# Expert inputs picked by matmuls with a zero-one matrix, in place of indirect gathers and transposes, in a one-core encoder step

## What is computed

```
g_idx = jnp.argmax(g_logits, axis=-1)                       # 1 of 4 groups
top_v, top_i = lax.top_k(e_sel, TOP_K_INNER)                # 2 of its 4 experts
top_w = jax.nn.softmax(top_v, axis=-1) * g_w
combine = jnp.sum(one_hot(e_idx, N_EXPERTS) * top_w[..., None], axis=1)
for e in range(N_EXPERTS):                                  # 16
    h = jax.nn.silu(xt @ w_gate[e]) * (xt @ w_up[e])        # 1024 -> 512
    y = y + combine[:, e:e + 1] * (h @ w_down[e])           # 512 -> 1024
```

## Time and profile before

| | us |
|---|---|
| Median of 3 runs | 639.69 (635.85 to 643.37) |
| The profiled execution, its own time | 645.62 |
| Its span, first to last instruction | 643.8 |
| Busy in the span: PE / PEld / DVE / ACT / POOL | 531.8 / 393.8 / 229.8 / 130.2 / 71.1 |
| Granted TensorE clock, mean of the span | 0.919 |
| Read from HBM in the execution | 146.14 MB |

### The profile page before, as it was taken

How to read it: one execution, slowest core, us unless ns; L and a number is a source line. 1 busy time by engine, 2 the same in 40 slices (tenths; PEclk the granted TensorE clock), 3 DMA queues, 4 the chain that set the end, 5 groups by cost and what they waited for, 6 DMA issues and landing times.

```text
span 643.8 us, 9041 instructions
## 1 busy us (share of the span) xinstructions
PE 531.8 (83%) x3544; PEld 393.8 (61%) x3545; DVE 229.8 (36%) x487; ACT 130.2 (20%) x240; POOL 71.1 (11%) x88
## 2 busy tenths in 40 slices
PE   1299979999999999999992699978987789787740
PEld 1299965987888897968772456544554455444310
DVE  5623985685344222213336111121111111111177
ACT  1424359654423122100020000000000000000010
POOL 4590400000000000010000700010000000000210
PEclk9999998977999999999975599998988999989795
DMA  7696541212135887891066269999999999999632
GB/s 216 193 235 224 150 131 54 84 61 65 34 131 186 312 281 273 285 329 69 33 254 252 80 255 374 389 398 393 390 386 412 409 408 406 409 424 424 236 122 82
DMA packets 55353, 158.53 MB, mean 246 GB/s; under 512 B 3572, under 2 KB 35792, under 8 KB 51216
## 3 DMA queue, kind: packets, MB, share of 16 engines
q1 hardware_dynamic: 46320, 135.11, 55.9%
q0 software_dynamic: 4896, 13.92, 8.0%
q10 hardware_dynamic: 4096, 8.92, 3.8%
HBM read 146.14 MB, written 11.78 MB: 245 GB/s over the span
## 4 chain that ended last, share of the span: by engine, by line
PE 61%; DMA 20%; DVE 7%; issue 4%; ACT 3%; SPq 3%; DVEq 0%; POOL 0%; POOLq 0%; ACTq 0%
PE bank L1015 19%; DMA expert_slots<-in_w_up 10%; PE bank L825 8%; PE bank L976 7%; PE bank L812 6%; PE bank L814 6%; PE bank L813 6%; DMA expert_slots<-in_w_in 5%; PE bank L901 3%; SPq L591 2%; PE bank L1008 2%; DMA z_rows<-work 2%; PE bank L881 1%; DVE work L1384 1%; DMA expert_slots<-expert_rows,slot_i 1%
## 5 line engine op out<-in xcount | busy, mean ns | idle before, releaser
L1015 PE MATMUL bank<-expert_slots,work 128*64 128x256 f32 (+3 forms) x1584 | 191.7, 416 | 26.1 <-DMA expert_slots<-in_w_gate 11.1
L1015 PEld LDWEIGHTS bank<-expert_slots,work 128*64 128x64 f32 (+1 forms) x1584 | 106.7, 139 | 100.0 <-issue 45.8
L812 PE MATMUL bank<-z_high,weights_high 128*128 128x320 f32 (+1 forms) x256 | 81.5, 318 | 0.6 <-DVE weights_low L532 0.6
L813 PE MATMUL bank<-z_low,weights_high 128*128 128x320 f32 (+1 forms) x256 | 79.9, 312 | 0.0
L814 PE MATMUL bank<-z_high,weights_low 128*128 128x320 f32 (+1 forms) x256 | 79.8, 312 | 0.0
L1720 DVE SCALAR_TENSOR_TENSOR work<-work,bank 128x256 f32<-128x256 f32 (+1 forms) x18 | 7.3, 406 | 144.0 <-ACT work L1296 138.1
L532 DVE TENSOR_TENSOR weights_low<-expert_slots,weights_high 128x2048 fp32r<-128x2048 f32 x18 | 41.2, 2287 | 34.0 <-ACT weights_high L527 34.0
L825 PE MATMUL bank<-work,expert_slots 128*128 128x320 f32 x192 | 52.3, 432 | 0.0
L812 PEld LDWEIGHTS bank<-z_high,weights_high 128*128 128x128 f32 x256 | 48.9, 191 | 1.9 <-DVE weights_low L532 1.1
L813 PEld LDWEIGHTS bank<-z_low,weights_high 128*128 128x128 f32 x256 | 48.6, 190 | 0.2
L814 PEld LDWEIGHTS bank<-z_high,weights_low 128*128 128x128 f32 x256 | 48.5, 189 | 0.0
(11 more groups left out here) (249 smaller groups left out, 590.8 us busy)
## 6 DMA issues: line engine op xcount, KB each, us to landing
expert_slots<-in_w_gate SPq DMA_DIRECT2D x16, 2048.0 KB, 25.0
expert_slots<-in_w_up SPq DMA_DIRECT2D x16, 2048.0 KB, 29.6
expert_slots<-in_w_down SPq DMA_DIRECT2D x15, 2048.0 KB, 23.5
expert_slots<-in_w_in SPq DMA_DIRECT2D x19, 1024.0 KB, 5.6
expert_slots<-in_w_branch_rnn SPq DMA_DIRECT2D x4, 1024.0 KB, 7.3
expert_slots<-in_w_out SPq DMA_DIRECT2D x4, 1024.0 KB, 5.7
expert_rows<-work ACTq DMA_DIRECT2D x30, 128.0 KB, 8.2
expert_rows<-work POOLq DMA_DIRECT2D x6, 384.0 KB, 9.3
```

What stands on the lines that cost most here:

```text
L812: nc.tensor.matmul(b[:, 0:NALL - lo], wh[:, k, o], zh[:, k, lo:NALL], start=(k == 0), stop=False)
L813: nc.tensor.matmul(b[:, 0:NALL - lo], wh[:, k, o], zl[k // 4][:, k % 4, lo:NALL], start=False, stop=False)
L1015: mm = nc.tensor.matmul(bank[m * j:m * j + m, cols], lhsT(k), rhs(k, j), start=(k == 0), stop=(k == kk - 1))
```

## The change

- `gather`, `turn` and the copies `columns` for the 16 experts go. TensorE forms an expert's input in `choose`: `rows` (stationary, every eighth column) times a matrix `pick` of tokens x places, zero or one, that VectorE makes (`pick_item`) from the token's rank plus one if it chose the expert (`pick_rank`). The product is already transposed. Only the first 64 places are made always; `choose_rest` makes the other 32 within the branch.
- `columns` copies one bank of 512 columns; `rest_columns` is added in the branch.
- The ranks take three matmuls in place of nine.
- The token index is made later (`overflow_index`), behind expert 0's turn of hidden, since only overflow items still gather.
- On VectorE `columns(0, 0)` stands amid the routing arithmetic; `pick_item(1)` and `(2)` behind the control words; its expert loop is written out; pick i + 3 is made behind `hidden_columns`.
- The multiplication of `rows` by ALPHA moves from Pool, early in the stage, to ACT, behind the last expert's tanh, because `rows` are now read until then. ACT waits for `ctrl_done` in its first step, not for `route_done` ahead of it.

```diff
-            for i in range(NE):
-                if i >= 3:
-                    pool.wait_ge(xt_full, i - 2)
-                gather(i, i % 3)
-                if i == 2:
-                    scale_residual()
...
-            for j in range(3):
-                for i in range(j):
-                    nc.tensor.matmul(b[:, NE * j:NE * j + NE], ones, e_sum[:, i, :], start=(i == 0), stop=False)
-                nc.tensor.matmul(b[:, NE * j:NE * j + NE], before, e_sum[:, j, :], start=(j == 0), stop=True)
-            for i in range(3):
-                mm = nc.tensor.matmul(b[:, NE * 3:NE * 4], ones, e_sum[:, i, :], start=(i == 0), stop=(i == 2))
...
+            nc.tensor.matmul(b[:, 0:NE], before, e_sum[:, 0, :], start=True, stop=True)
+            nc.tensor.matmul(b[:, NE:4 * NE], ones, e_upto.rearrange(flat), start=True, stop=False)
+            nc.tensor.matmul(b[:, NE:3 * NE], before, e_sum[:, 1:3, :].rearrange(flat), start=False, stop=True)\
+                .then_inc(S.f_full("ranks"), 1)
...
+            def picked(bank, s, at, n):
+
+                for k in range(KD):
+                    for j in range(3):
+                        m = OUT_ROWS[j]
+                        z = rows[0:m, j, :].rearrange("t (p k) -> t k p", k=KD)
+                        mm = nc.tensor.matmul(bank[:, n * k:n * k + n], z[:, k, :], pick[s][0:m, j, at:at + n],
+                                              start=(j == 0), stop=(j == 2))
+                return mm
+
+            def choose(i, s):
+
+                pe.wait_ge(pick_made, i + 1)
                 wait_past(pe, xt_made, i)
+                picked(TB[0], s, 0, FIRST).then_inc(xt_full, 1)
+
+            def choose_rest(s, b):
+
+                picked(TB[1], s, FIRST, REST).then_inc(xr_full, 1)
+                pe.wait_ge(xr_made, b + 1)
...
                     hidden(i, s, n, ha_full)
                     if not (first and s == 0):
                         down(i - 1, (s - 1) % 3, n if s else n - 1)
-                    turn(i + 1, (s + 1) % 3, n + (s + 1) // 3)
+                    choose(i + 1, (s + 1) % 3)
+                    if first and s == 0:
+                        pe.wait_ge(ctrl_done, 1)
+                    if first and s == 1:
+                        pe.wait_ge(route_done, 1)
                     maybe_rest(i, s, n)
                     turn_hidden(ha_made, i + 1, hta_full)
-
-            turn(0, 0, 0)
+                    if first and s == 0:
+                        overflow_index()
+
+            choose(0, 0)
...
+            for j in range(3):
+                n = OUT_ROWS[j]
+                nc.scalar.mul(rows[0:n, j, :], rows[0:n, j, :], ALPHA).then_inc(rows_scaled2, 1)
...
+            def pick_item(i):
+
+                slot = cst("iota_cap").unsqueeze(1).to_broadcast([P, 3, CAP])
+                mine = pick_rank[:, :, i].unsqueeze(2).to_broadcast([P, 3, CAP])
+                stt(pick[i % 3], slot, 1.0, mine, ALU.add, ALU.is_equal).then_inc(pick_made, 1)
+
+            def columns(i, s):
+                dve.wait_ge(xt_full, i + 1)
+                V.tensor_copy(xT[s][:, :, 0:FIRST], TB[0][:, :].rearrange("p (k c) -> p k c", c=FIRST)).then_inc(xt_made, 1)
```

More of the change, by code:

```diff
@@ L233, in pe_fills @@
         s += [(kind, j, h) for h in range(2)]
-    s += ["ranks", "index"]
+    s.append("ranks")
     return m, s
@@ L350, in build @@
         ea = Area(work, 3 * D, NWORK)
-        xg = [ea.take(D) for _ in range(3)]
+        pick = [ea.take(3, CAP) for _ in range(3)]
+        xg = ea.take(D)
         xT = [ea.take(KD, CAP) for _ in range(3)]
@@ L384, in build @@
         br = sb("router_bias", [1, 20])
-        rt = Area(work, 3 * D + KD * (NALL + META) + KD * NTOK + 4 * NTOK, NWORK)
+        rt = Area(work, max(ea.at, 3 * D + KD * (NALL + META) + KD * NTOK + 4 * NTOK), NWORK)
         logit = rt.take(3, 20)
-        e_sum = rt.take(3, NE)
+        e_sum, e_upto = rt.take(3, NE), rt.take(3, NE)
         rank_hot = rt.take(2, 3 * CAP)
@@ L393, in build @@
         own = sm.take(2, 3)
+        pick_rank = sm.take(3, NE)
         idle = sm.take(1)
@@ L991, in _ @@
-            pe.wait_ge(selected, 1)
-            b = S.claim(pe, "index")
-            for k in range(2):
-                for j in range(3):
-                    mm = nc.tensor.matmul(b[0:CAP, 0:NITEM], rank_hot[:, k, CAP * j:CAP * j + CAP], item_hot[:, k, NITEM * j:NITEM * j + NITEM],
-                                          start=(k == 0 and j == 0), stop=(k == 1 and j == 2))
-            mm.then_inc(S.f_full("index"), 1)
-            pe.wait_ge(route_done, 1)
-            def turn(i, s, n):
-                pe.wait_ge(xg_in[s], 16 * (n + 1))
-                wait_past(pe, xt_made, i)
-                cols = xg[s][0:CAP, :].rearrange("c (p k) -> c k p", k=KD)
+            flat = "p j e -> p (j e)"
@@ new lines, in _, with overflow_index @@
+            nc.tensor.matmul(b[:, 0:NE], before, e_sum[:, 0, :], start=True, stop=True)
+            nc.tensor.matmul(b[:, NE:4 * NE], ones, e_upto.rearrange(flat), start=True, stop=False)
+            nc.tensor.matmul(b[:, NE:3 * NE], before, e_sum[:, 1:3, :].rearrange(flat), start=False, stop=True)\
+                .then_inc(S.f_full("ranks"), 1)
+            def overflow_index():
+                pe.wait_ge(selected, 1)
+                for k in range(2):
+                    for j in range(3):
+                        mm = nc.tensor.matmul(TB[1][0:CAP, 0:NITEM], rank_hot[:, k, CAP * j:CAP * j + CAP],
+                                              item_hot[:, k, NITEM * j:NITEM * j + NITEM],
+                                              start=(k == 0 and j == 0), stop=(k == 1 and j == 2))
+                mm.then_inc(index_full, 1)
@@ L1336, in round_of @@
                         rows_out(i - 1, (s - 1) % 3, n if s else n - 1, i - 1)
+                    if first and s == 0:
+                        act.wait_ge(ctrl_done, 1)
                     maybe_rest(i)
@@ L1668, in _ @@
             step.settle()
+            columns(0, 0)
             alone(stt(base, ov_end, float(NE - 1), ov, ALU.add, ALU.subtract))
@@ L1783, in _ @@
             with dve.If(has > 0):
+                rest_columns(0, b)
                 rest(b + count)
```

80 lines of the change are left out of this document (45 added, 35 removed).

## The result

The changed kernel takes 869.75 us (861.56 to 870.67, 4 runs) beside 641.53 us (635.85 to 644.36, 4 runs) of the kernel before, measured on the same chip: a ratio of 1.353, 95% interval 1.346 to 1.359. The direction was as predicted, the size was not: 714 us had been forecast, with 738 as the upper end.

What follows compares the result with a forecast made beforehand. TensorE's pace was taken to bound the early expert stage, the weight stream the later. 86.1 + 15.5 - 26.7 - 1.4 = +73.5 us, added to the median 639.7, gave 713.2, plus 1 more: 714, range 668 to 738.

Steps and rivals of the forecast that it cites:

- Price of one choose: TensorE's 48 records forming one expert's input: 7.55 us against 1.07 for the transposes before; 6.9 us for a rest.
- the first of the three prices: In a choose, each record's load of 128 columns was to take 107 to 112 ns, taken from L954.
- rival C: Choose loads pay for reading every eighth word: 224 ns a load, 13.1 us a choose, 812 us in all; chance 0.12.
- The clock: Expert matmuls in each step of the stage were priced at 10.56 us, with a choose of 7.55 at full clock.
- Start of the stage: Ranks to expert 1: choose(0) 10.2 us, 5.3 of it at half clock; expert 1 at 373.9 instead of 375.30, saving 1.4.
- the change of rows: In a choose, switching between 128 and 64 rows adds about 40 ns and leaves the second record's load unhidden: 200, then 160.
- the copy: VectorE's copy behind each choose: one of 512 columns, 0.78 us instead of 1.10.
- the tail behind expert 14: From the end of expert 14's down matmuls to the end of the span: 45 us, as before.
- ScalarE's scaling: Residual scaling moved behind the last tanh, ending at 616.3, costed at nothing; about 1 us without cover.
- The break-even of 3.4 us a choose: Choose time at which the kernel's time would be unchanged: 3.4 us, 71 ns a record.
- that nothing but TensorE's own records could be late: In the expert stage, steps of 18.89 us on TensorE exceed the weight stream's 15.8 us an expert, so only TensorE is late.
- the 26.7: Expert stage of the kernel before: 26.7 us taken as waits for weights and slower clock behind them, which would go.

Runs made afterwards that it cites:

- e2: Changed kernel with the loaded columns read at steps of 1, 2, 4 and 8 words, two of the eight groups each; 818.4 us.
- e7: Changed kernel with each pick moved four times over, 256 columns in place of 64, into the same columns; 884.25 us, ratio 1.379.
- e1: Changed kernel with the 128 columns of each load side by side instead of eight words apart; 807.19 us, ratio 1.259.
- e11: e10 with the gate and up matmuls of the rest joined, shortening the loop's turn and the jump; 654.25 us, ratio 1.016.
- e8: Changed kernel with one of the eight groups of matmuls in each choose, the others left out; 628.53 us, ratio 0.974.
- e9: Kernel before with the cheaper ranks and expert 0's input formed by matmul as in e10, gathers for the other experts; 636.79 us, ratio 0.990.
- e12: e10 with the expert's own gate and up matmuls joined, the rest's code as long as in e10; 666.49 us, ratio 1.031.
- e6: e5 with the rest's code and words taken out of TensorE, ScalarE and VectorE for experts 0 to 14; 661.4 us, ratio 1.032.
- e5: e4 with the branch for more than 64 rows never taken, its code left in place; 754.92 us, ratio 1.178.
- e4: Changed kernel with contiguous loads and 128 rows in all three matmuls of a group; 776.6 us, ratio 1.209.
- e10: Changed kernel with pick matmul sides exchanged: zero-one matrix loaded, rows moved, 12 records instead of 48, four transposes behind; 705.36 us, ratio 1.099.

## Why the prediction was wrong, step by step

The forecast of the span was 643.8 + 73.5 = 717.3 us; the profiled one is 868.7, that is 151.4 more. Read off the chain:

- **Price of one choose.** The fourteen chooses of the stage with the two pieces for rests take 226.3 us, not 14 x 7.55 + 2 x 6.9 = 119.5: +106.8. The failed step is the first of the three prices, the load at 112 ns: it is 237 in this shape. I took it from L954, whose columns lie side by side, and let L1008's transposes stand for what a step of eight words can cost; in e2 the step alone doubles the price of a pick's load. The 134 ns that rival C reads there are 1.07 us over eight; in the trace of before, the starts of these transposes (in the group at 385.80 us) lie 110 to 114 ns apart behind the first, so that they pay nothing for the step. Why a transpose of rows read at the same step escapes it, no run here shows: a nearest row has to match in kind of operation as well as in step. Rival C had the mechanism and 13.1 us a choose (13.6 at the full clock measured), and I gave it 0.12.
- **The clock.** The sum took 10.56 us for an expert since the earlier trace rows has 0.95 in the stage. Over 14 experts it is 170.1 instead of 147.8: +22.2. The forecast never asked whether TensorE could be full of work and still be slowed; the changed kernel shows that it can, and e7 that moving more columns keeps the clock up. Rival C's 812 lacked this too.
- **Start of the stage.** Expert 1 at 384.8 instead of 373.9: +10.9, the same two prices in choose(0), choose(1) and expert 0. The sum let the clock rise after 5.3 us of choose(0), which stood at 0.50 for all of its 14.5 us. Against this stand 3.0 us by which the first pick came earlier than I had it (343.34 for 346.35).
- **The remainder**, 11.5 us: mainly four gaps of 1.0 to 1.4 us (three where a turn of the loop ends, one ahead of the last down matmuls), the rests' matmuls (5.4 and 5.6 for 3.67 us) and the last down matmuls (6.63 for 3.67) at the lower clock, and 1.7 in the tail.

What held: no wait for weights is left; the change of rows (205/160/201 measured for 200/160/200, e1); the copy, 0.85 for 0.78; the tail behind expert 14, 47.0 for 45.3 us; and ScalarE's scaling hidden. The break-even of 3.4 us a choose isn't borne out: e11, with 2.72 us for the picks and 0.6 for four transposes, is 1.6% slower than before, and e8, with 1.7 us, is 2.6% faster, so it lies between, as far as kernels that differ in more than this can tell. What fell besides: that nothing but TensorE's own records could be late. The longer code is a cost that the diff doesn't show. The trace of before had a sign of it: the gap of 3.8 us at 431.82 and the slower matmuls behind it, 5.8 us together, are in the 26.7 that the forecast took for waits for weights.

Also open: which property of the turn's code sets the bound between 393 and 441 matmuls (bytes or their place in memory), and why single gaps of 2.9 to 4.7 us remain ahead of expert 1 in e9, e11 and e12, where the loop hasn't begun. Code that has to be brought in once, when it is first run, would fit them and the gaps of before, e8 and e12 ahead of the loop and in its first turn; no run tests it.

## What to carry to other kernels

In a matmul that selects or permutes, load the small matrix and move the long one; the f32 words to be loaded should lie one or two words apart, since at steps of four and eight each load of such a matmul costs double. A high busy share of TensorE doesn't vouch for its clock: read the granted clock in each half of a step. And count the instructions of a loop's turn before adding to it, branches that are never taken included: the queue of code in the profile shows whether the turn is still kept.

## What I had not expected of the hardware

- A load of 128 f32 columns for a pick takes 112, 118, 234 and 238 ns at steps of 1, 2, 4 and 8 words (e2 and the changed kernel); the last two are the same at either clock, the first two are 213 ns at half. The transposes of before, also at a step of 8, follow each other at 110 to 114 ns.
- The clock fell to 0.5 in the midst of unbroken TensorE work (the changed kernel, e1) and came back only some us into the matmuls behind it; in the plain steps of e7 and e6 it stayed at 1.00. The first choose of e7, which began at 0.50, stayed there for 25.7 us.
- Code never executed, with the reading of its words, cost 93.5 us (e5 to e6), and some 8 packets of 16 KB came in with each turn. In most steps with such a gap, other than where a turn ends, it was 10.1 to 11.1 us from the start of the choose to the next matmul behind the jump (e1, e4, e5, e10); some took 8.4 to 8.9 (e10), one 11.6 (e1). The Trainium skill, "Runtime: NRT & Kernel Launch", section "Instruction fetch mechanics", says that a taken branch out of the code at hand has to wait for a fetch; the gaps of e4 and e10 agree, and e8, e11 and e12 show that a turn of the loop short enough is spared it.
